# A two-layer hybrid model on one core: the weight buffers are staggered by 64 bytes, other operands start on multiples of 512 bytes

## The reference, cut to what matters

```python
def first_block(x, ...):
    for l in range(2):
        x = x + 0.5 * swiglu(rms_norm(x, ffn1_norm[l]), ffn1_w_gate[l], ffn1_w_up[l], ffn1_w_down[l])  # 1024x2816 x2, 2816x1024
        u = rms_norm(x, mix_norm[l]) @ w_in[l]
        z, xbc, dt_raw, q_lat, kv_lat, k_pe, c_h, c_b, c_c = jnp.split(u, pts, axis=-1)
        y_ssd, y_mla, y_conv = ssd_mixer(...), mla_mixer(...), conv_mixer(...)
        x = x + jnp.concatenate([y_ssd, y_mla, y_conv], axis=-1) @ w_out[l]                            # 2048x1024
        x = x + 0.5 * swiglu(rms_norm(x, ffn2_norm[l]), ffn2_w_gate[l], ffn2_w_up[l], ffn2_w_down[l])
    return x

def hybrid_layer(x, ...):            # second block, two layers
    proj = rmsnorm(x, norm_g) @ w_in                                                                   # 1024x10256
    ...                              # differential attention, mLSTM, gates
    u = jax.nn.sigmoid(ga) * ya + jax.nn.sigmoid(gb) * yb
    return x + u @ w_o
```

## The kernel before

| tensor | phase before |
|---|---|
| X, XTH, XTL, RAW and WL (all slots), WH (all slots), CONSTS | 128 |
| FR | 320 |
| HTB | 448 |
| H | 320 |

## Time and profile before

### The profile page before, as it was taken

One profiled execution on the slowest core, in us unless ns is written; L12 is line 12 of the kernel. 1 busy time (PEld: TensorE's weight loads), 2 busy tenths in 40 slices (PEclk: granted clock), 3 DMA queues, 4 the chain that ended last, 5 costly groups with the idle time before them and its releaser, 6 DMA issues.

```text
span 1860.9 us, 24686 instructions
## 1 busy us (share of the span) xinstructions
PE 1846.2 (99%) x9674; PEld 1561.2 (84%) x9674; DVE 1219.5 (66%) x1872; ACT 1059.2 (57%) x1559; POOL 98.0 (5%) x85
## 2 busy tenths in 40 slices
PE   9999999999999999999999999999999999999999
PEld 7888998788888888899888888888878888887887
DVE  5654697865555555588876555587767567875745
ACT  6444667565444444476756444575776456568642
POOL 0000110000000000020000000002001000210100
PEclk9999999999999999999999999999999999999999
DMA  7555543345555555553325555554445545534553
GB/s 289 188 185 179 176 155 102 114 136 182 190 183 192 181 183 190 181 182 114 125 91 170 185 188 184 169 191 148 136 139 179 192 162 184 176 120 139 172 188 117
DMA packets 86580, 309.83 MB, mean 166 GB/s; under 512 B 9648, under 2 KB 10288, under 8 KB 86464
## 3 DMA queue, kind: packets, MB, share of 16 engines
q1 hardware_dynamic: 85680, 306.35, 49.7%
q0 software_dynamic: 496, 1.65, 0.2%
q10 hardware_dynamic: 288, 0.25, 0.0%
HBM read 307.16 MB, written 1.05 MB: 166 GB/s over the span
## 4 chain that ended last, share of the span: by engine, by line
PE 95%; ACT 3%; DVE 1%; issue 0%; DMA 0%; POOL 0%; SPq 0%; DVEq 0%; ACTq 0%
PE bank L1131 91%; PE bank L1128 4%; ACT PA L1550 1%; DVE PA L2619 0%; ACT MP L1550 0%; ACT WH L1550 0%; ACT L1550 0%; DVE WL L2002 0%; DMA X<-in_x_dram 0%; ACT ET L1550 0%; DVE PC L2644 0%; DVE STATS L2317 0%; ACT BZ L1550 0%; DVE BO L2609 0%; DVE X L2088 0%
## 5 line engine op out<-in xcount | busy, mean ns | idle before, releaser
L2002 DVE TENSOR_TENSOR WL<-RAW,WH 128x1024 fp32r<-128x1024 f32 x585 | 704.9, 1213 | 441.1 <-ACT WH L1550 436.4
L1550 ACT ACTIVATE WH<-RAW 128x1024 fp32r<-128x1024 f32 (+2 forms) x587 | 609.7, 1049 | 454.5 <-PE bank L1131 451.1
L1131 PE MATMUL bank<-WH,XTH 128*128 128x512 f32 (+1 forms) x1376 | 392.1, 396 | 0.6 <-ACT XTH L1550 0.6
L1131 PE MATMUL bank<-WH,XTL 128*128 128x512 f32 (+1 forms) x1376 | 381.9, 389 | 0.0
L1131 PE MATMUL bank<-WL,XTH 128*128 128x512 f32 (+1 forms) x1376 | 381.3, 389 | 0.0
L1131 PE MATMUL bank<-WH,FR 128*128 128x512 f32 x1264 | 320.4, 392 | 0.0
L1131 PEld LDWEIGHTS bank<-WH,XTL 128*128 128x128 f32 x1376 | 258.2, 188 | 54.4 <-DVE XTL L2015 0.2
L1131 PEld LDWEIGHTS bank<-WL,XTH 128*128 128x128 f32 x1376 | 258.3, 188 | 53.2
L1131 PEld LDWEIGHTS bank<-WH,XTH 128*128 128x128 f32 x1376 | 252.0, 188 | 52.4 <-issue 5.7
L1131 PEld LDWEIGHTS bank<-WH,FR 128*128 128x128 f32 x1264 | 233.8, 188 | 49.5 <-issue 0.8
L1131 PE MATMUL bank<-WL,FR 128*128 128x512 f32 x632 | 174.4, 390 | 0.0
(11 more groups left out here) (317 smaller groups left out, 1606.6 us busy)
## 6 DMA issues: line engine op xcount, KB each, us to landing
RAW<-in_WALL_dram SPq DMA_DIRECT2D x569, 512.0 KB, 3.3
RAW<-in_WALL_dram SPq DMA_DIRECT2D x8, 448.0 KB, 3.3
RAW<-in_WALL_dram SPq DMA_DIRECT2D x8, 256.0 KB, 2.7
X<-in_x_dram SPq DMA_DIRECT2D x4, 256.0 KB, 5.1
out_dram<-X SPq DMA_DIRECT2D x4, 256.0 KB, 2.0
ROWP<-in_ROWP_dram POOLq DMA_DIRECT2D x1, 672.0 KB, 10.6
CONSTS<-in_CST_dram POOLq DMA_DIRECT2D x1, 664.0 KB, 8.2
ROUNDED<-in_CSTR_dram POOLq DMA_DIRECT2D x1, 208.0 KB, 13.5
```

The costliest lines, as they stand in the source:

```text
L1131: return self.e.matmul(out, lhs, rhs, start=start, stop=stop, skip_group_check=True)
L1550: return self.e.activation(out, in_, func, **k)
L2002: self.e.tensor_tensor(lo, raw, hi.bitcast(F32), ALU.subtract).then_inc(*self.up("lo", j))
```

## The change

The order of the tensors in SBUF is new. CONSTS, COLP, ROWP, STATS, SUMS, SPREAD and ROUNDED come first; X then starts at byte 32768, and XN, XTH, XTL and RAW follow directly. A slot of RAW, WL and WH is now `BLK + 16` elements long, 4160 bytes, of which the last 64 are never used. The arena starts on a multiple of 512 bytes, and JUNK moves into XN. One DMA names `0:BLK` of its slot, since a slot is longer now. No instruction, wait, semaphore or DMA is added or removed, and none changes its place in any engine's stream: between the two programs every engine has the same instructions in the same order, on other addresses.

```diff
 class Kernel: def allocate(self):
         self.top = (self.nc.sbuf_base + 31) // 32 * 32
-        self.X = self.fixed("X", [128, 2, D])
-        self.xn_at = self.top
-        self.XN = self.fixed("XN", [128, 2, D])
-        self.xt_at = self.top
-        self.XTH = self.fixed("XTH", [128, 8, S], F32R)
-        self.XTL = self.fixed("XTL", [128, 8, S], F32R)
-        self.WL = self.nc.alloc_sbuf_tensor_at("WL", [128, NRAW, BLK], F32R, offset=self.top)
-        self.RAW = self.fixed("RAW", [128, NRAW, BLK])
-        self.WH = self.fixed("WH", [128, NSPLIT, BLK], F32R)
         self.C = self.fixed("CONSTS", [128, NCONST])
...
+        self.R = self.fixed("ROUNDED", [128, 416], F32R)
+        assert self.top % 2048 == 0
+        self.X = self.fixed("X", [128, 2, D])
+        self.xn_at = self.top
+        self.XN = self.fixed("XN", [128, 2, D])
+        self.XTH = self.fixed("XTH", [128, 8, S], F32R)
+        self.XTL = self.fixed("XTL", [128, 8, S], F32R)
+        self.WL = self.nc.alloc_sbuf_tensor_at("WL", [128, NRAW, BLK + 16], F32R, offset=self.top)
+        self.RAW = self.fixed("RAW", [128, NRAW, BLK + 16])
+        self.WH = self.fixed("WH", [128, NSPLIT, BLK + 16], F32R)
+        self.top += -self.top % 512
+        self.arena0 = self.top
+        self.top += 108704
         self.HM = self.fixed("HALFS", [128, 16])
         self.ROPE = self.fixed("ROPE", [128, 2, 96])
...
+        self.JUNK, _ = self.arena("JUNK", [128, 512], 4096, mybir.dt.bfloat16, base=self.xn_at)
...
-        assert h <= 32768
-        h = 32768
+        assert h <= 32640
+        h = 32640
         self.VA, _ = mk("VA", [128, 2, D], h)
...
 class Sync: def program(self):
-                e.dma_start(k.RAW[:, 1, :], second).then_inc(*k.sig.landed("raw1", 1))
+                e.dma_start(k.RAW[:, 1, 0:BLK], second).then_inc(*k.sig.landed("raw1", 1))
```

More of the change, by code:

```diff
@@ L895, in allocate @@
         self.ST = self.fixed("STATS", [128, 288])
+        self.SS = self.fixed("SUMS", [128, 72])
+        self.SPREAD = self.fixed("SPREAD", [128, 128])
+        self.R = self.fixed("ROUNDED", [128, 416], F32R)
[11 more added lines that the diff above has]
+        self.top += 108704
         self.HM = self.fixed("HALFS", [128, 16])
         self.ROPE = self.fixed("ROPE", [128, 2, 96])
[L898 to L903, removed]
+        self.JUNK, _ = self.arena("JUNK", [128, 512], 4096, mybir.dt.bfloat16, base=self.xn_at)
         c = self.C
```

## The result

The changed kernel takes 1879.07 us (median of 4 runs, 1878.78 to 1879.37) against 1863.13 us for the kernel before in the same session. The ratio is 1.0084, 95% interval 1.0072 to 1.0097. The forecast was 1872.9 with a range of 1850 to 1890: right in sign and cause, but nearly two fifths too small in size (+9.8 us forecast, +15.9 measured).

The account below looks back on a forecast made before the run. TensorE, busy 99% of the span, was taken as the bound, so only product durations matter. Terms +13.7 - 0.9 + 2.2 - 0.6 - 4.6 = +9.8 us on 1860.9, plus 2.2 outside the span, gave 1872.9 us; range 1850 to 1890.

Parts of the forecast that it names:

- D: Phase (address modulo 512) of the moving operand minus that of the stationary one loaded beside it; claimed to set product duration.
- Part 1: 4032 products of 512 columns against XTH and XTL: 226.6 to 230 ns, +13.7 us, less 0.9 already disturbed by transposes.
- my mean: Part 1's first estimate for 512 columns: levels 226.6, 228.8, 233.3 and the mixed 232.0 averaged to 230.2 ns.
- the unsettled value: Part 1's second estimate: 230 ns, seen behind transposes before TensorE settles at D = 0 after some seven products.
- Part 2: 512-column products against FR (1872) and HTB (192), both going to 230 ns: +2.2 us and -0.6 us.
- Part 3: 1536 products of 256 columns with weights stationary: 120.0 to 117 ns each, -4.6 us.
- Part 4: All but weight products (transposes, ScalarE and VectorE preparation, weight DMA): 0 us, ends -1 and +2.
- Rival 1: Faster: wide products settle at the floor for most D, narrow ones gain; about 1851 us, chance 0.27.
- Rival 2: No change: phases do not matter between TensorE's two reads, or both signs cancel; 1863 us, chance 0.12.
- Rival 3: An unmeasured D costs over 6.7 ns, or changes prevent settling; 235 ns average, 1900 us or more, chance 0.08.
- Rival 4: Far faster: the floor itself is a collision of TensorE's two reads that some D avoids; 1782 us, chance 0.02.
- The signs named beforehand: Changed profile: 44 products about 10.1 us, slot 0 near 226.6 ns, FR and HTB at XTH's mean, eight narrow about 0.94 us.

Follow-up runs that it names:

- flat0: Changed kernel without the stagger: slots of RAW, WL and WH back to 4096 bytes, large operands at phase 0; 1857.89 us against 1862.83 before, ratio 0.9973.
- lower_at_128: flat0 with RAW and WL moved 128 bytes on, so D is 0 over WH and 128 over WL in every block; 1873.65 us.
- d32x480x96: Changed kernel with 4096-byte slots at phase 0 and activations moved to constant D of 32 (XTH), 480 (FR), 96 (HTB); 1892.76 us.

## Why the prediction was right, point by point

- **What bounds the kernel.** Right: TensorE stayed at 99% with no new wait, and the whole change lies in the durations of its products. ScalarE and VectorE moved by 1 ns and by nothing.
- **D as the cause.** Right, and now shown: with the weight slots fixed and the activations moved, every tensor takes the rate of its D. The modulus was wrong. The three phases at hand (0, 192, 320) could not tell 256 from 512, and I took the 512 of the layout.
- **Part 1, wide products against XTH and XTL: +12.8 us forecast, +15.9 measured.** This is the term that was too small. With the levels now known, the passes over WH average 229.8 and that over WL 230.5, together 230.1, which is the 230 that I took. That was partly luck. One of the four numbers in my mean, 232.0 from the 448-column rows, I had read as a mix of D = 0 and 256; but at 512 columns both are at the floor, and the 448-column products take 203 ns in flat0 too. It happens to lie beside the 232.5 of D = 128. What failed is the next step: the changes of D add to the levels, and I had used the unsettled value as another estimate of the same thing, not as a term of its own. The changed kernel has a mean of 231.1, 1.0 ns over its levels; by slot the excess is 2.4 to 3.2 ns at D = 0 and 256 and nothing at 128 and 192. By levels and changes, the stagger costs 6096 x (230.1 - 227.1) = 18 us and, with the 1.1 ns of lower_at_128, 7 us over the flat layout, less 2.8 us of narrow products: 22 us, measured 21.2. The kernel before was itself some 5 us over the flat layout.
- **Part 2: FR +2.2 forecast, +3.7 measured; HTB -0.6 and -0.4.** The same error of about 1 ns: 231.1 in place of 230.
- **Part 3: -4.6 forecast, -2.6 measured.** Taken 117, measured 118.0. The 113.3 of one short stretch was a settled rate at one D, and the narrow products seldom get there.
- **Part 4: nothing.** Right: transposes of H at 272, of X at 273, weight DMA waits of 1.9 us.
- **Rivals.** Rival 1 asked that the wide products settle at the floor for most D. They do so at 0 and 256 alone of the twelve values tried. Rival 2, and with it the rule of two independent ports of the Trainium skill ("TensorE: Matmul & The Clock Gate", "Step-by-step: what each phase is for"), does not hold for these float32r products: with the weight slots in place and only XTH, XTL and the arena shifted, the span was 1855.8 us (flat0) or 1891.0 (d32x480x96). Rival 3 did not come: the mean is 231.1, not 235. But a D that costs over 6.7 ns exists, 160 at 234.2; the stagger does not use it. Rival 4: no D has a mean under 226.7.
- **The signs named beforehand.** The 44 products take 10.12 us (about 10.1 forecast); products against XTH, FR and HTB come to the same mean (231.3, 231.2 and 231.3 ns); eight narrow ones to 0.944 us (0.94). One sign failed: slot 0 was to stay near 226.6 and is at 229.5, and that is the missing term.

What stays open is the mechanism below D: why 32 bytes are as bad as 192, why the 448-column products do not follow, and why there are two settled rates for 256 columns. Nor does any run tell whether it is a product's own weight load or the next one's, which runs beside it, that matters: the two have the same phase nearly everywhere. No run here looks into that.

## What to carry to other kernels

When TensorE is the bound, measure the distance between the starts of equal products for each pair of tensors before touching anything else: two rates for one shape, with clock and waits alike, can be an address effect, and moving one tensor tells. For float32r products with a weight load each, as here, let the moving operand and the stationary one that is loaded beside it begin at equal addresses modulo 256 if the moving one has 512 columns, for all slots and all products, so that nothing has to settle anew; a pitch of slots that is a multiple of 256 keeps it. With 256 columns a shift helps a little, and what it gives depends on where the engine settles, so it must be measured.

## What the runs showed of the hardware that was not expected

- The duration of a 512-column float32r product with its weight load depends on D modulo 256: 226.7 ns settled and a mean of 227.1 at 0, a mean of 229 at 64, 233.3 at 32, 233.4 at 96, 232.5 at 128, 234.2 at 160, 233.3 at 192, 233.2 at 224. That is up to 3% of TensorE's time, with all clocks and waits the same.
- After a change of D it takes some seven products to settle (lower_at_128: 231 to 233 ns for three, 227.1 at the eighth); with a change every two to eight products the cost is 1.0 to 1.5 ns per product on top of the levels.
- The transposes of H in float32 (272 to 273 ns), VectorE's subtraction (1223 to 1224 ns mean) and ScalarE's rounding (1059 to 1060) were the same in all of these layouts. The transposes of X have a mean of 272 to 273 in nine of the kernels and 277 to 278 in five. In the one of the five that I looked at closely, lower_at_128, three single transposes of the 128 with 213 to 240 ns to the next start make the difference; the median from start to start is 109 ns in every kernel.
